# Attention stage: probabilities as the stationary operand of the values' product, division on the way out, key copies moved

## The reference

```python
def one_chunk(args):                      # prompt
    sc = jnp.einsum('blhd,bmhd->bhlm', qc, kb) * scale + bias
    sc = jnp.where(valid, sc, -jnp.inf)
    p = jax.nn.softmax(sc, axis=-1)
    return jnp.einsum('bhlm,bmhd->blhd', p.astype(vb.dtype), vb)
# streams: the same with k_all = [cache_k, ka], v_all = [cache_v, va], bias by relative distance
```

## Time and profile before

| | |
|---|---|
| median of 3 runs | 2030.17 us (2026.6 to 2032.75) |
| span of the profiled execution | 2028.7 us; no other time of it is shown |
| PE, weight loads, DVE, ACT, POOL busy | 96%, 87%, 37%, 31%, 29% |
| attention's main loop | from 610.4 to about 784 us |

### The profile page before, as it was taken

How to read it: one execution, slowest core, us unless ns; L and a number is a source line. 1 busy time by engine, 2 the same in 40 slices (tenths; PEclk the granted TensorE clock), 3 DMA queues, 4 the chain that set the end, 5 groups by cost and what they waited for, 6 DMA issues and landing times. The chain is left out here.

```text
span 2028.7 us, 34282 instructions
## 1 busy us (share of the span) xinstructions
PE 1945.0 (96%) x14050; PEld 1759.9 (87%) x14050; DVE 746.8 (37%) x1482; ACT 634.4 (31%) x1283; POOL 590.6 (29%) x456
## 2 busy tenths in 40 slices
PE   7999999999998888899799999999999999999998
PEld 7899999999994566678699879999999999999997
DVE  5211777111125664565553182222222222222225
ACT  5101222100016664344443245222222222222222
POOL 3111111111132002543354144333333333333333
PEclk9999999999998998999899999999999999999999
DMA  4322223522227213131253232111111111111114
GB/s 119 108 89 88 76 88 118 209 88 88 88 97 238 92 64 84 44 96 39 62 158 105 104 125 88 47 43 42 42 42 42 42 42 42 42 42 42 42 60 169
DMA packets 159273, 169.22 MB, mean 83 GB/s; under 512 B 14187, under 2 KB 130043, under 8 KB 159150
## 3 DMA queue, kind: packets, MB, share of 16 engines
q1 hardware_dynamic: 152814, 141.52, 22.7%
q10 hardware_dynamic: 6336, 25.96, 3.2%
HBM read 126.84 MB, written 40.55 MB: 83 GB/s over the span
## 5 line engine op out<-in xcount | busy, mean ns | idle before, releaser
L2369 DVE TENSOR_TENSOR t_acc<-t_acc,t_B 128x512 f32<-128x512 f32 x252 | 173.3, 688 | 538.6 <-PE t_B L2475 538.6
L116 PE MATMUL i_ps<-x_hi,i_w_lo 128*128 128x384 f32 x1008 | 337.5, 335 | 0.0
L116 PE MATMUL i_ps<-x_hi,i_w_hi 128*128 128x384 f32 x1008 | 337.2, 335 | 0.0
L116 PE MATMUL i_ps<-x_lo,i_w_hi 128*128 128x384 f32 x1008 | 337.2, 335 | 0.0
L2462 PE MATMUL t_B<-t_merged_hi,t_wm_lo 128*128 128x384 f32 x768 | 256.9, 335 | 1.0 <-POOL t_wm_lo L2052 1.0
L2462 PE MATMUL t_B<-t_merged_lo,t_wm_hi 128*128 128x384 f32 x768 | 256.6, 334 | 0.0
L2462 PE MATMUL t_B<-t_merged_hi,t_wm_hi 128*128 128x384 f32 x768 | 256.6, 334 | 0.0
L106 POOL TENSOR_TENSOR i_w_lo<-i_w_raw,i_w_hi 128x1024 fp32r<-128x1024 f32 x44 | 105.4, 2395 | 433.4 <-ACT i_w_hi L101 433.4
L2052 POOL TENSOR_TENSOR t_wm_lo<-t_raw,t_wm_hi 128x1024 fp32r<-128x1024 f32 x49 | 118.8, 2425 | 295.9 <-ACT t_wm_hi L2127 295.9
L116 PEld LDWEIGHTS i_ps<-x_lo,i_w_hi 128*128 128x128 f32 x1008 | 189.8, 188 | 0.0
L116 PEld LDWEIGHTS i_ps<-x_hi,i_w_lo 128*128 128x128 f32 x1008 | 189.7, 188 | 0.0
(11 more groups left out here) (344 smaller groups left out, 3465.9 us busy)
## 6 DMA issues: line engine op xcount, KB each, us to landing
proj<-i_out ACTq DMA_DIRECT2D x44, 576.0 KB, 2.8
i_w_raw<-in_w_in SPq DMA_DIRECT2D x44, 512.0 KB, 3.9
t_raw<-in_w_up SPq DMA_DIRECT2D x32, 512.0 KB, 4.2
t_raw<-in_w_down SPq DMA_DIRECT2D x32, 512.0 KB, 3.6
t_gates<-proj SPq DMA_DIRECT2D x48, 192.0 KB, 2.7
a_k_cache<-in_cache_attn_k SPq DMA_DIRECT2D x8, 1024.0 KB, 6.1
a_v_cache<-in_cache_attn_v SPq DMA_DIRECT2D x8, 1024.0 KB, 5.3
d_c<-proj SPq DMA_DIRECT2D x3, 1536.0 KB, 7.6
```

What stands on the lines that cost most here:

```text
L116: last = pe.matmul(out, a[s][:, c, :], b[:, c, tokens], start=k == 0, stop=k == n - 1)
L2369: dve.tensor_tensor(a, a, B[(ND * j + d) % 4][:, :], ALU.add).then_inc(added, 1)
```

## The change

- `values_pair`: the turned probabilities become the stationary operand (128 columns), the values move (64 columns). The result stands with queries on partitions, head 0 in columns 0 to 63 and head 1 in 64 to 127.
- `recip` keeps only the reciprocal, in a ring of 18 columns. The multiplication of the probabilities is gone; `turn` waits for the exponential. `out` now multiplies O by the reciprocal of each query on its way to `sy` (or `so` for the stream) and stands first in DVE's step.
- `turn_result` transposes `sy` or `so` into a new bank TY; `result` on DVE copies it to `env.oa`, between the two `soft` of an even step.
- S is one tensor of three banks instead of two of two, to make room for TY. With five blocks both heads of a pair have columns in the middle bank; their products are cut anew and one waits for another (`s_edge`). `soft` of a pair's first head waits for both heads, and the stream's scores wait for all units before.
- DVE instead of ACT copies the turned cache keys (`key`).
- The schedule: values at the steps 1, 3, 4, 5, 7 of a round (before 1, 3, 4, 6, 8), results one step later, keys at 1, 3, 5 and 7 (the last for the next round). Within a step PE's order is scores, turn, keys, result, values.

```diff
-        nmax, rsum, rinv = sb("nmax", [P, SR]), sb("rsum", [P, SR]), sb("rinv", [P, SR])
+        nmax, rsum, rinv = sb("nmax", [P, SR]), sb("rsum", [P, SR]), sb("rinv", [P, 2 * STEP])
+        sy = [sb(f"result{i}", [P, 2, AD]) for i in range(2)]
...
-        S = [c.enter_context(nc.psum_tensor(f"a_S{i}", [P, 1024], F32)) for i in range(2)]
+        S = c.enter_context(nc.psum_tensor("a_S", [P, 1536], F32))
...
-        TK, O = (c.enter_context(nc.psum_tensor(f"a_{name}", [P, 512], F32)) for name in ("TK", "O"))
+        TK, TY, O = (c.enter_context(nc.psum_tensor(f"a_{name}", [P, 512], F32)) for name in ("TK", "TY", "O"))
...
+        def first_col(h, n):
+            return 0 if h % 2 == 0 else 1536 - n * P
...
+        def values_at(st):
+            b, h = divmod(st, STEP)
+            u = {1: STEP * (b - 1) + 4, 3: STEP * (b - 1) + 6, 4: STEP * (b - 1) + AH, 5: STEP * b, 7: STEP * b + 2}.get(h, -1)
+            return u if 0 <= u < NU else None
+        def result_at(st):
+            h = st % STEP
+            return values_at(st - 1) if h in (2, 4, 5, 6, 8) else None
+        def key_at(st):
+            b, h = divmod(st, STEP)
+            if st == 0:
+                return 0
+            if h == AH - 1 and b + 1 < NB:
+                return 4 * (b + 1)
+            return 4 * b + (h + 1) // 2 if b < NB and h in (1, 3, 5) else None
...
 # DVE, recip
-                dve.wait_ge(r_made, u + 1)
-                x = s[r][:, 0:keys_of(u)[2] * P if prompt(u) else KEYS]
-                dve.tensor_scalar(x, x, rinv[:, r:r + 1], None, ALU.mult).then_inc(p_scaled, 1)
 # DVE, out
+                    dve.tensor_tensor(sy[u % STEP // 2 % 2][:, :, :], O[:, 0:P].rearrange("p (w d) -> p w d", w=2),
+                                      bc(inverse(u), 2, AD), ALU.mult).then_inc(av_read, 1)
...
+                    dve.tensor_scalar(so[:, :], O[:, 0:P], inverse(u), None, ALU.mult).then_inc(av_read, 1)
 # DVE, result
+                    dve.tensor_copy(env.oa[:, h // 2, b * P:(b + 1) * P], TY[:, 0:P]).then_inc(ty_read, 1)
...
+            def key(j):
+                b, pair = divmod(j, 4)
+                dve.wait_ge(tk_made, j + 1)
+                if b >= 2:
+                    dve.wait_ge(s_made, stream(b - 2) + 1)
+                dve.tensor_copy(kt[b % 2][:, pair, :], TK[:, :]).then_inc(tk_read, 1)
 # PE, scores_pair
+                if edge:
+                    part(1, 0, P).then_inc(s_edge, 1)
+                    part(0, 0, 512)
+                    part(1, P, W).then_inc(s_made, 1)
+                    pe.wait_ge(s_edge, 4 * (b - 4) + h // 2 + 1)
+                    part(0, 512, W).then_inc(s_made, 1)
+                else:
+                    part(0, 0, W).then_inc(s_made, 1)
+                    part(1, 0, W).then_inc(s_made, 1)
 # PE, turn
-                pe.wait_ge(p_scaled, u + 1)
+                pe.wait_ge(p_made, u + 1)
 # PE, results
+            def turn_result(u):
+                pe.wait_ge(av_read, group(u) + 1)
+                if u:
+                    pe.wait_ge(ty_read, group(u))
+                src = sy[u % STEP // 2 % 2][:, :, :].rearrange("p w d -> p (w d)") if prompt(u) else so[:, :]
+                pe.transpose(TY[:, 0:P], src, env.ident[:, :]).then_inc(ty_made, 1)
 # PE, values_pair
-                for i in range(n):
-                    for w in range(2):
-                        last = pe.matmul(O[AD * w:AD * w + AD, 0:P],
-                                         vt[:, k0 // P + i, (h + w) * AD:(h + w + 1) * AD],
-                                         turned_p(u + w)[:, i * P:(i + 1) * P], start=i == 0, stop=i == n - 1)
+                for w in range(2):
+                    for i in range(n):
+                        last = pe.matmul(O[:, AD * w:AD * w + AD], turned_p(u + w)[:, i * P:(i + 1) * P],
+                                         vt[:, k0 // P + i, (h + w) * AD:(h + w + 1) * AD], start=i == 0, stop=i == n - 1)
```

More of the change, by code:

```diff
@@ L669, in group, with inverse @@
             return 5 * (u // STEP) + u % STEP // 2
-        def side_jobs(st):
-            b, h = divmod(st, STEP)
[L674 to L682, removed]
+        def first_col(h, n):
+            return 0 if h % 2 == 0 else 1536 - n * P
+        def inverse(u):
+            b, h = divmod(u, STEP)
+            a = STEP * (b % 2) + h
+            return rinv[:, a:a + 1 + (h < AH)]
+        def values_at(st):
+            b, h = divmod(st, STEP)
+            u = {1: STEP * (b - 1) + 4, 3: STEP * (b - 1) + 6, 4: STEP * (b - 1) + AH, 5: STEP * b, 7: STEP * b + 2}.get(h, -1)
[10 more added lines that the diff above has]
+            return 4 * b + (h + 1) // 2 if b < NB and h in (1, 3, 5) else None
+        STEPS = NU + AH
         @block.sync
@@ L692, in load_k @@
                 if b >= 2:
-                    sp.wait_ge(tk_made, side["K", 4 * (b - 2) + 3] + 1)
+                    sp.wait_ge(tk_made, 4 * (b - 2) + 4)
                 sp.dma_start(kc[b % 2][:, :, :], I["cache_attn_k"][0, b].rearrange("(t p) h d -> p t (h d)", p=P)
@@ L822, in turned @@
                     act.activation(turned_p(u)[:, n:KEYS], TR[:, n:KEYS], ACT.Copy).then_inc(tr_read, 1)
[L824 to L836, removed]
             for st in range(STEPS):
@@ L848, in _ @@
                                    accum_out=rsum[:, st % SR:st % SR + 1]).then_inc(p_made, 1)
-                for j in side_jobs(st):
-                    side_out(j)
         @block.vector
@@ L872, in soft @@
                 r = u % SR
-                x, ps = s[r], S[u % 2]
-                dve.wait_ge(s_made, u + 1)
+                x = s[r]
+                b, h = divmod(u, STEP)
+                dve.wait_ge(s_made, u + 2 - u % STEP % 2 if prompt(u) else u + 1)
                 if u >= SR:
@@ L879, in soft @@
                 if prompt(u):
-                    b, h, n, _ = keys_of(u)
-                    W = n * P
+                    n = keys_of(u)[2]
+                    W, a = n * P, first_col(h, n)
                     if n > 2:
                         dve.wait_ge(far_made, 1)
-                    dve.tensor_tensor_reduce(x[:, 0:W], ps[:, 0:W], bias[:, h, KEYS - W:], -SC, -NEG, ALU.add, ALU.min,
+                    dve.tensor_tensor_reduce(x[:, 0:W], S[:, a:a + W], bias[:, h, KEYS - W:], -SC, -NEG, ALU.add, ALU.min,
                                              least).then_inc(s_read, 1)
                 else:
-                    b = u // STEP
                     if b == 0:
@@ L891, in soft @@
                         dve.wait_ge(far_made, 2)
-                    dve.tensor_tensor_reduce(x[:, 0:REACH], ps[:, 0:REACH], bias_s[:, 0:REACH], -SC, -NEG, ALU.add, ALU.min,
+                    dve.tensor_tensor_reduce(x[:, 0:REACH], S[:, 0:REACH], bias_s[:, 0:REACH], -SC, -NEG, ALU.add, ALU.min,
                                              part[:, 0:1]).then_inc(s_part, 1)
@@ L896, in soft @@
                         dve.wait_ge(bias_made, 3)
-                    dve.tensor_tensor_reduce(x[:, REACH:KEYS], ps[:, REACH:KEYS], bias_own[:, P - TS - TS * b:2 * P - TS - TS * b], -SC, part[:, 0:1],
+                    dve.tensor_tensor_reduce(x[:, REACH:KEYS], S[:, REACH:KEYS], bias_own[:, P - TS - TS * b:2 * P - TS - TS * b], -SC, part[:, 0:1],
                                              ALU.add, ALU.min, least).then_inc(s_read, 1)
             def recip(u):
-                r = u % SR
+                b, h = divmod(u, STEP)
@@ L914, in out, with result @@
+            def result(u):
+                b, h = divmod(u, STEP)
+                dve.wait_ge(ty_made, group(u) + 1)
+                if prompt(u):
+                    if u == 0:
                         for sem, n in env.proj_sent:
                             dve.wait_ge(sem, n)
-                    b, h = divmod(u, STEP)
-                    dve.tensor_copy(env.oa[:, h // 2, b * P:(b + 1) * P], O[:, 0:P]).then_inc(av_read, 1)
-                else:
-                    if u >= STEP:
-                        dve.wait_ge(tk_made, side["X", u // STEP - 1] + 1)
-                    dve.tensor_copy(so[:, :], O[:, 0:P]).then_inc(av_read, 1)
+                    dve.tensor_copy(env.oa[:, h // 2, b * P:(b + 1) * P], TY[:, 0:P]).then_inc(ty_read, 1)
+                else:
+                    stood = TY[:, 0:P].rearrange("p (j w q) -> p j w q", w=2, q=TS)
+                    dve.tensor_copy(env.oa[0:64, :, TP + TS * b:TP + TS * (b + 1)], stood[0:64, :, 0, :])
+                    dve.tensor_copy(env.oa[64:P, :, TP + TS * b:TP + TS * (b + 1)], stood[64:P, :, 1, :]).then_inc(ty_read, 1)
@@ L923, in _ @@
+            def key(j):
+                b, pair = divmod(j, 4)
+                dve.wait_ge(tk_made, j + 1)
+                if b >= 2:
+                    dve.wait_ge(s_made, stream(b - 2) + 1)
+                dve.tensor_copy(kt[b % 2][:, pair, :], TK[:, :]).then_inc(tk_read, 1)
             for st in range(STEPS):
-                if st < NU and (st % STEP % 2 == 0 or not prompt(st)):
+                u = result_at(st)
```

(61 more changed lines are left out.)

26 lines of the change are left out of this document (16 added, 10 removed).

## The result

The changed kernel takes 2048.38 us in the median of 4 runs (2044.28 to 2053.46), the kernel before 2031.46 beside it (2026.6 to 2034.57): ratio 1.0084, 95% interval 1.0061 to 1.0108, so 12 to 22 us slower. The profiled span is 2044.1 us against 2028.7.

What follows compares the result with a forecast made beforehand. PE's in-order queue was taken as the bound. Rounds, head and end summed 3 x 4.6 + 4.4 + 2.3 + 0.9 - 0.8 - 0.5 + 1.5 = 21.6; 2028.7 + 21.6 + 1.5 = 2051.8 us, range 2038 to 2061.

Steps and rivals of the forecast that it cites:

- the signs named: Signs of being right: values loads about 2.3 us, rounds 28 to 29, scores to turning 1.6, no 1.4 wait, VectorE's share lower.
- Part one: Values' product: each of 480 passes rises from 0.0545 to 0.112 us, set by the weight load; +1.17 a five-block pair.
- rival A: Values' product: moving columns set the pace, so 480 x 0.0575 = 27.6 us less, 2024 us; chance 0.09.
- Part two: Five-block scores in the shared PSUM bank: odd head's 512 columns end 0.32 us later, 16 pairs, 5.1 us.
- rival B: Five-block scores: the two halves still overlap fully, 5.1 us less, 2046.7 us; chance 0.17.
- wait (b): Before the stream's values: PE waits 1.43 us until VectorE empties O behind two softmax reductions; forecast to go.
- end +1.5: End of the stage: two values' products +2.3 us, waits for ScalarE and for O less 0.8.
- Part three: Division, keys, results: VectorE stays near 15 us of a round, no bound; 40 results add one 0.11 transpose each.
- the third turn wait: Between turn(3) and turn(4), where values no longer stand: a new wait, +0.7 us a five-block round.
- the softmax wait: Start of the round: scores(0) wait for the stream's softmax, +0.6 us a five-block round.
- Rivals C and D: C: results between VectorE's reductions delay scores, 2060, chance 0.10; D: removed waits give more, about 2040, chance 0.08.
- E: Rival: the 1.2 GHz stretch at the beginning goes or grows, 3 us either way, inside the range, no chance of its own.

Runs made afterwards that it cites:

- in two experiments: Each against the kernel before: the swapped values' product alone, 2052.82 us; key copies on DVE instead of ACT alone, 2039.16 us.
- in a third: The changed kernel with the values' product of before put back, 2030.39 us, ratio 0.9982.

## Why the prediction was right, and where it was off

The forecast was 2052 (+21.6), the range 2038 to 2061; measured 2048.4 (+17). Right were the direction and what causes it, the price of the product. The number is nearer than the sum deserves: the sum was for this stage, and there 14.1 was measured, not 21.6. The rest of the 17 are 1.3 outside the stage and 1.5 between profiled run and medians, and neither comes from the change as far as is known. Of the signs named, 2.3 us of loads and the missing wait of 1.4 came; a round of 28 to 29 and 1.6 from scores to turning did not (27.04 and 1.29), and VectorE's share stayed at 37%.

- Part one, the values' product: right in mechanism and size. A pass costs 0.111 (2.31 us for 20 loads), found from two rows of shapes that were not the same; the two experiments on moving and loaded columns show that it is the load. The Trainium skill's rule in TensorE: Matmul & The Clock Gate, LDWEIGHTS (loading the stationary operand), some 107 ns for 128 columns, agrees with the 0.111 of this trace. The isolated gap from the moving columns, which the Trainium skill gives on the same page under Back-to-back issue gap, would have led to rival A, which the runs exclude. The Trainium skill's advice to swap and use two column tiles (TensorEngine Tiling (Array Packing), When to Use Tiling) is borne out by the +3.76 a round that undoing it costs here.
- Part two, the five-block scores, +0.32 a pair: wrong, it is 0 to 0.01 (1.28 before, 1.29 after). This was rival B, given a chance of 0.17. In the new order, too, a pass of one row half starts between the two passes of a product on the other half: the odd head's 512 columns start at 742.76, the even head's second pass at 742.98. The step that failed is "can't begin before the even head's second pass has". Of the sum's 21.6, 5.1 go with it. The prediction said that no row showed such overtaking, in the same paragraph as its own remark that the two halves ran side by side. The program issues head 0's product before head 1's, each of two passes, and the four loads within 0.30 us at 732.68 are those of both heads, so it had been there.
- The round: 28.72 listed, 27.04 measured. 1.28 of the difference are the scores; the rest are gaps between full-array work, 0.50 from turning to keys (0.55 listed) and 2.37 for a product (2.41). The new waits stand where they were listed: 0.65 before scores(0), 0.71 before turn(4); wait (b) is gone.
- Other rounds, forecast and measured: 4: 27.7, 26.04; 3: 23.0, 22.62; 2: 19.3, 18.99; 1: 16.5, 17.09. Head -0.5, measured -0.85; end +1.5, measured +1.65. The last full round is 26.62, as one group of key transposes, for a round that does not come, falls away, which I had not taken off. Round 1 is near by luck: its 16.5 held 0.9 for a low clock that did not come (1.00), so 15.6 is what to compare, and it took 1.5 more. The early key transpose did wait for its cache load, longer than the 1 us left in the range:

```profile
637.88 0.42 PEld L1055 LDWEIGHTS a_TK<-ident,a_k_cache 128*128 128x128 f32 x4 [1.64 <-issue]
637.91 0.63 PE L1055 MATMUL a_TK<-ident,a_k_cache 128*128 128x128 f32 x4 [1.44 <-DMA a_k_cache<-in_cache_attn_k]
```

- Part three: right that division and copies are no bound. Without the product the change gains 3.7 us (0.4 to 6.9); O emptied first alone gains 6.5 (2.2 to 10.8). These two intervals overlap, but the rounds tell them apart: 23.29 against 22.82, both at 1.00. So what else the change does takes 0.47 of a round back; the third turn wait and the softmax wait in the rows above are candidates. How it divides between them was not tried one by one.
- Rivals C and D did not show. E did: before, the head and round 1 ran at granted clocks of 0.68 and 0.90, after at 1.00, and yet the profile gives no separate price, since the head fell by only 0.85.

## What to carry to other kernels

Swapping the operands of a product exchanges moving columns for loaded ones. With fp32 and 128 loaded columns a pass cost 0.11 us here whether 64 or 128 columns moved, so halving the moving side gains nothing, and two column halves side by side are lost. Where one engine's in-order queue is the bound, look for work that fits into its waits (two groups of four transposes for nothing) and for the buffer whose reader stands too late in another engine's step, rather than for work to take off engines with room.

## What the hardware showed beyond that

- The two passes of an fp32 product leave room for passes of a product on the other row half. In each of the 16 five-block pairs the four products start 0, 0.01, 0.33 and 0.97 us into the pair, the second pass of the second one at 0.54, behind the start of the third. So the scores take 1.29 us in an order for which the prediction, with passes one behind the other, had 1.6. The Trainium skill (TensorE: Matmul & The Clock Gate, The mechanism) has products start and end in program order; counted as whole products they do so here, and the trace does not speak against it. It was the prediction's step from products to passes that did not hold.
- No idle time stands between the weight loads of turnings, keys and the swapped product, which all use the whole array, while 0.17 stands between a turning and a product with 64 or 32 loaded columns. By the starts of the loads that pays back 0.2 of each swapped product.
- The stretch at 1.2 GHz in the first rounds differs from kernel to kernel: round 1's clock was 0.90 before, 1.00 after, 0.61 and 0.64 in two experiments, where it took 22.4 and 21.6 us instead of 17; in a third it was round 2 that had 0.75 and took 21.6 instead of 18.5. What each engine does there before it was not tried apart, and stays open; I therefore compare rounds at 1.00.
